# First attention of a hybrid encoder layer: inverse row sums by way of DRAM, another order of the key halves, value products between the scores and both turned tiles

## The reference, cut to what matters

```python
logits = jnp.einsum('bhqd,bhkd->bhqk', q_i, k).astype(jnp.float32) * scale
logits = logits + c_i[..., :, None] - cum[..., None, :]
logits = jnp.where(pos_i[:, None] >= kpos[None, :], logits, -jnp.inf)
p = jax.nn.softmax(logits, axis=-1)
return jnp.einsum('bhqk,bhkd->bhqd', p.astype(v.dtype), v)
```

## Time and profile before

| what | value |
|---|---|
| median of 3 runs | 1885.44 us (1884.57 to 1885.84) |
| the profiled execution | 1884.72 us, of which its span is 1883.0 us |
| PE busy in the span | 1855.8 us (99%) |
| DVE, ACT, POOL busy | 1180.3 us (63%), 765.0 us (41%), 842.1 us (45%) |
| pair 1: first `scores` of pair 1 to that of pair 2 | 801.94 to 852.30, 50.36 us |
| last `normalise` of pair 3 ends | 942.76 us |

### The profile page before, as it was taken

How to read it: one execution, slowest core, us unless ns; L and a number is a source line. 1 busy time by engine, 2 the same in 40 slices (tenths; PEclk the granted TensorE clock), 3 DMA queues, 4 the chain that set the end, 5 groups by cost and what they waited for, 6 DMA issues and landing times.

```text
span 1883.0 us, 25321 instructions
## 1 busy us (share of the span) xinstructions
PE 1855.8 (99%) x9100; PEld 1527.1 (81%) x9100; DVE 1180.3 (63%) x1763; ACT 765.0 (41%) x1439; POOL 842.1 (45%) x635
## 2 busy tenths in 40 slices
PE   7999999999999999999999999999999999999998
PEld 6888888888888878777788888878888888888886
DVE  6966777676777882555604567486534454368778
ACT  5633233332444552555513555353333323334445
POOL 1688877883000111222222332699877887700003
PEclk8999999999999999999999999999999999999999
DMA  9247566654976301301112123524322422178662
GB/s 355 87 140 214 180 209 198 192 167 150 397 226 197 116 24 51 138 18 44 68 56 63 48 65 134 175 89 134 105 91 92 133 99 98 46 295 313 208 190 90
DMA packets 213363, 267.95 MB, mean 142 GB/s; under 512 B 16084, under 2 KB 126840, under 8 KB 212728
## 3 DMA queue, kind: packets, MB, share of 16 engines
q1 hardware_dynamic: 212392, 263.72, 42.2%
q10 hardware_dynamic: 848, 2.62, 0.4%
HBM read 211.17 MB, written 53.03 MB: 140 GB/s over the span
## 4 chain that ended last, share of the span: by engine, by line
PE 88%; POOL 4%; DVE 4%; issue 2%; ACT 1%; DMA 1%; SPq 0%; DVEq 0%; ACTq 0%; POOLq 0%
PE bank L1772 13%; PE bank L1774 13%; PE bank L1773 13%; PE bank L1200 7%; PE bank L1199 7%; PE bank L1201 6%; PE bank L2136 5%; PE bank L2138 5%; PE bank L2137 5%; PE bank L2907 2%; PE bank L2891 2%; PE bank L2876 1%; POOL out_xn L157 1%; PE bank L3304 1%; PE bank L3303 1%
## 5 line engine op out<-in xcount | busy, mean ns | idle before, releaser
L510 POOL TENSOR_TENSOR ffn_ring_b<-ffn_raw_in,ffn_ring_b 128x512 fp32r<-128x512 f32 x146 | 205.6, 1416 | 97.6 <-ACT ffn_ring_b L505 97.5
L1199 PE MATMUL bank<-ffn_w_hi,ffn_a_hi 128*128 128x512 f32 x616 | 239.7, 389 | 0.0
L1201 PE MATMUL bank<-ffn_w_hi,ffn_a_lo 128*128 128x512 f32 x616 | 239.6, 389 | 0.0
L1200 PE MATMUL bank<-ffn_w_lo,ffn_a_hi 128*128 128x512 f32 x616 | 239.6, 389 | 0.0
L132 POOL TENSOR_SCALAR rms<-rms 128x1 f32<-128x1 f32 x20 | 9.0, 450 | 427.6 <-ACT ffn_junk L124 419.6
L1154 ACT CAST ffn_a_hi<-ffn_a_stage 128x512 fp32r<-128x512 f32 x154 | 95.7, 621 | 200.8 <-PE bank L1201 196.9
L505 ACT CAST ffn_ring_b<-ffn_raw_in 128x512 fp32r<-128x512 f32 x150 | 92.5, 621 | 201.9 <-PE bank L1774 195.9
L510 POOL TENSOR_TENSOR ffn_ring_a_lo<-ffn_raw_in,ffn_ring_a_hi 128x512 fp32r<-128x512 f32 x106 | 146.6, 1394 | 54.0 <-ACT ffn_ring_a_hi L505 51.9
L1165 DVE TENSOR_TENSOR ffn_a_lo<-ffn_a_stage,ffn_a_hi 128x512 fp32r<-128x512 f32 x154 | 106.5, 691 | 71.9 <-ACT ffn_a_hi L1154 71.9
L1551 DVE TENSOR_TENSOR ffn_u<-bank,ffn_u 128x512 f32<-128x512 f32 x103 | 70.9, 689 | 109.6 <-PE bank L1774 109.1
L2128 POOL TENSOR_TENSOR mx_w_lo<-mx_raw_w,mx_w_hi 128x1024 fp32r<-128x1024 f32 x25 | 59.8, 2391 | 176.8 <-ACT mx_w_hi L1890 113.3
(11 more groups left out here) (427 smaller groups left out, 4686.9 us busy)
## 6 DMA issues: line engine op xcount, KB each, us to landing
ffn_raw_in<-in_w_ffn_in SPq DMA_DIRECT2D x84, 512.0 KB, 5.8
ffn_a_stage<-hidden SPq DMA_DIRECT2D x154, 256.0 KB, 3.4
ffn_w_stage<-in_w_ffn_out SPq DMA_DIRECT2D x132, 256.0 KB, 3.1
ada_rest<-in_w_ada SPq DMA_DIRECT2D x64, 448.0 KB, 3.9
hidden<-ffn_u SPq DMA_DIRECT2D x87, 256.0 KB, 2.0
hidden<-ffn_g SPq DMA_DIRECT2D x66, 256.0 KB, 2.0
mx_raw_w<-in_w_mix_in SPq DMA_DIRECT2D x28, 512.0 KB, 4.5
x_spill<-xres SPq DMA_DIRECT2D x16, 512.0 KB, 5.6
```

Of the source, the lines that this page charges most:

```text
L510: pool.tensor_tensor(self.lo(q), self.source(b, m), self.hi(q).bitcast(F32), ALU.subtract)\
L1199: pe.matmul(dst, a_hi, w_hi, start=first, stop=False, skip_group_check=True)
L1200: pe.matmul(dst, a_hi, w_lo, start=False, stop=False, skip_group_check=True)
L1201: return pe.matmul(dst, a_lo, w_hi, start=False, stop=True, skip_group_check=True)
```

## The change

Three things are changed together.

1. **The division.** DVE takes the inverse of two numbers per query (128x2) into a table `mx_rinv` of 128 queries by 16. At the end of a pair it transposes the table in 32x32 blocks. SP writes it to DRAM in four small DMAs and reads it back spread over the partitions in two (`spread_inverse`), and POOL multiplies the whole pair's result, 128x1024, in place (`divide`): for pairs 0 to 2 at step 4 of the next pair, for pair 3 after the weight cuts and ahead of the memset of `mx_mask_m`. `turn_rinv` and `keep_rinv` are gone; DVE copies the undivided value product (`keep_y_fox`).
2. **The key halves.** The low half of the keys (g = 2) is projected after step 6 and the high half (g = 3) last. `scores(0)` waits for each half of the keys ahead of its own matmuls. Since the low half is still read by `scores(7)` of the pair before, ACT waits for that ahead of its copy.
3. **The order on PE.** In steps 2 to 5 too, `values(q-2)` stands ahead of both turned tiles.

```diff
@@ -2079,7 +2081,11 @@
-    rinv = core.at("mx_rinv", [P, 4, P], 120)
+    TURN = 32
+    rinv = core.at("mx_rinv", [P, TURN], 120)
+    rinv_rows_in = core.at("mx_rinv_rows_in", [P, TURN], 120.5)
+    rinv_bc = core.at("mx_rinv_bc", [P, S], 16)
+    rinv_rows = nc.dram_tensor("rinv_rows", (PAIRS * 2 * S,), F32, kind="Internal").ap()
@@ -2186,8 +2192,8 @@
     BLOCK = [NS - 1 - n // 2 for n in range(PER)]
-    STEP_OF = {5: 1, 6: 3, 7: 2}
-    QK_ORDER = (1, 3, 2, 0)
+    STEP_OF = {5: 1, 6: 2, 7: 3}
+    QK_ORDER = (1, 2, 3, 0)
@@ -2199,7 +2205,7 @@
-        return core.bank[:, (7, 1, 1, 3)[g], :]
+        return core.bank[:, (7, 1, 3, 1)[g], :]
@@ -2216,6 +2222,21 @@
+
+        def spread_inverse(pairs):
+
+            before = pairs - 1
+            sp.wait_ge(rinv_turned, pairs)
+            rows = rinv_rows[bass.ds(before * (2 * S), 2 * S)].rearrange("(n t) -> n t", t=P)
+            for at in range(0, P, TURN):
+                sp.dma_start(rows[:, at:at + TURN], rinv_rows_in[at:at + 2 * NS, :]).then_inc(rinv_stored, 16)
+            sp.wait_ge(rinv_stored, pairs * (P // TURN * 16))
+            sp.wait_ge(x_spilled, NS * 16)
+            if pairs > 1:
+                sp.wait_ge(y_divided, pairs - 1)
+            for e in range(2):
+                sp.dma_start(rinv_bc[e * HD:(e + 1) * HD, :],
+                             rinv_rows[bass.ds(before * (2 * S) + e * S, S)].partition_broadcast(HD)).then_inc(rinv_loaded, 16)
@@ -2225,13 +2246,19 @@
                     w_load(sp, slot, p + (C_F[slot] + 1), w_in[:, :, bass.ds(p * P + (col + P), P)])
+            if not first and not last:
+                spread_inverse(p)
             if first:
 ...
-        repeat(sp, PAIRS, fox_loads)
+        for p in range(PAIRS):
+            fox_loads(p, p == 0, p == PAIRS - 1)
         for piece in range(4):
             w_load(sp, piece % 2, C_MV[0] + piece // 2, w_in[:, 2 * piece:2 * piece + 2, COL_MV:COL_MV + MW])
+            if piece == 1:
+                spread_inverse(PAIRS - 1)
+        spread_inverse(PAIRS)
@@ -2291,9 +2318,18 @@
+        def divide(pairs):
+
+            part = yT_fox[:, bass.ds(pairs + -1, 1), :].rearrange("p a s -> p (a s)")
+            pool.wait_ge(y_done, pairs * NS)
+            pool.wait_ge(rinv_loaded, pairs * 32)
+            pool.tensor_tensor(part, part, rinv_bc[:, :], ALU.mult).then_inc(y_divided, 1)
+
 ...
                 mask_block(p, q)
+                if q == 4 and not first:
+                    divide(p)
                 if q in (1, 2):
@@ -2318,7 +2354,7 @@
-        pool.wait_ge(y_done, PAIRS * NS)
+        divide(PAIRS)
         pool.memset(mask_m[:, :], 0.0).then_inc(late_mask_set, 1)
@@ -2377,6 +2413,8 @@
             else:
+                if g == 2 and not (isinstance(p, int) and p == 0):
+                    act.wait_ge(score_ready, p * PER)
                 act.copy(fk_hi[:, half], qk_bank(p, g)).then_inc(fq_kept, 1)
@@ -2395,12 +2433,6 @@
-
-        def keep_rinv(p, q, first):
-            act.wait_ge(pv_ready, p * NS + (q + 1))
-            if not (first and q < 2):
-                act.wait_ge(y_done, p * NS + (q - 1))
-            act.copy(rinv[:, 2 + q % 2, :], core.bank[:, 6 + q % 2, P:2 * P]).then_inc(rinv_kept, 1)
@@ -2420,11 +2452,8 @@
                         keep_qk(p + 1, STEP_OF[q - 1])
-                if q > 1:
-                    keep_rinv(p, q - 2, first)
                 if q < NS:
                     keep_pt(p, 2 * q - 1, first)
-            keep_rinv(p, NS - 1, first)
             if not last:
@@ -2613,17 +2643,17 @@
             dve.wait_ge(prob_done, p * PER + (2 * q + 2))
-            if not (first and q < 2):
-                dve.wait_ge(pv_ready, p * NS + (q - 1))
-            dve.reciprocal(rinv[:, q % 2, :].rearrange("p (e d) -> p e d", e=2),
-                           rowsum[:, 2 * q:2 * q + 2].unsqueeze(2).to_broadcast([P, 2, HD]))\
-                .then_inc(rinv_made, 1)
-
-        def normalise(p, q):
-            dve.wait_ge(rinv_kept, p * NS + (q + 1))
             i = BLOCK[2 * q]
-            dve.tensor_tensor(yT_fox[:, bass.ds(p, 1), i * P:(i + 1) * P].rearrange("p a s -> p (a s)"),
-                              core.bank[:, 6 + q % 2, 0:P], rinv[:, 2 + q % 2, :], ALU.mult).then_inc(y_done, 1)
+            inverse = rinv[:, 0:2 * NS].rearrange("p (e i) -> p e i", e=2)[:, :, i:i + 1]
+            if q == 0 and not first:
+                dve.wait_ge(rinv_turned, p)
+            dve.reciprocal(inverse, rowsum[:, 2 * q:2 * q + 2].unsqueeze(2)).then_inc(rinv_made, 1)
+
+        def keep_y_fox(p, q):
+            dve.wait_ge(pv_ready, p * NS + (q + 1))
+            i = BLOCK[2 * q]
+            dve.tensor_copy(yT_fox[:, bass.ds(p, 1), i * P:(i + 1) * P].rearrange("p a s -> p (a s)"),
+                            core.bank[:, 6 + q % 2, 0:P]).then_inc(y_done, 1)
@@ -2642,8 +2672,12 @@
                 if q > 1:
-                    normalise(p, q - 2)
-            normalise(p, NS - 1)
+                    keep_y_fox(p, q - 2)
+            dve.wait_ge(rinv_made, p * NS + NS)
+            if not first:
+                dve.wait_ge(rinv_stored, p * (P // TURN * 16))
+            dve.transpose(rinv_rows_in[:, :], rinv[:, :]).then_inc(rinv_turned, 1)
+            keep_y_fox(p, NS - 1)
             if not last:
@@ -2652,6 +2686,8 @@
         dve.tensor_copy(m_max[:, :], max_turned_bank[:, FH * NS:]).then_inc(max_kept, 1)
+        dve.memset(rinv[:, :], 0.0).then_inc(rinv_set, 1)
+        dve.wait_ge(rinv_set, 1)
         repeat(dve, PAIRS, fox_body)
@@ -2820,9 +2856,9 @@
         def project_qk(p, g, ks=range(KD)):
-            if g % 2:
+            if g in (1, 2):
                 pe.wait_ge(w_lo_done[g // 2], p + (C_F[g // 2] + 1))
-            if g == 2 and ks[0] == 0:
+            if g == 3 and ks[0] == 0:
                 pe.wait_ge(fq_cut, p * 4 + 1)
@@ -2859,16 +2895,16 @@
             heads = [slice(e * HD, (e + 1) * HD) for e in range(2)]
-            if q == 0:
-                pe.wait_ge(fq_cut, p * 4 + 3)
-                if first:
-                    pe.wait_ge(rows_kept, 2)
+            if q == 0 and first:
+                pe.wait_ge(rows_kept, 2)
             if BLOCK[2 * q] == NS // 2 - 1:
 ...
                 k0, k1 = b * BANK, min((b + 1) * BANK, w)
+                if q == 0:
+                    pe.wait_ge(fq_cut, p * 4 + (2 + b))
@@ -2904,13 +2940,9 @@
                 for e in range(2):
-                    pe.matmul(bank[e * HD:(e + 1) * HD, 0:P], v_fox[:, j, bass.ds(p * (2 * HD) + e * HD, HD)],
-                              pt_of(2 * q + e, j * P, (j + 1) * P), start=(j == 0), stop=(j == i))
-
-        def turn_rinv(p, q):
-            bank = core.bank[:, 6 + q % 2, :]
-            pe.wait_ge(rinv_made, p * NS + (q + 1))
-            pe.transpose(bank[:, P:2 * P], rinv[:, q % 2, :], core.ident[:, :]).then_inc(pv_ready, 1)
+                    mm = pe.matmul(bank[e * HD:(e + 1) * HD, 0:P], v_fox[:, j, bass.ds(p * (2 * HD) + e * HD, HD)],
+                                   pt_of(2 * q + e, j * P, (j + 1) * P), start=(j == 0), stop=(j == i))
+            mm.then_inc(pv_ready, 1)
@@ -2922,17 +2954,12 @@
                 scores(p, q, first)
-                if q in (6, 7):
+                if q > 1:
                     values(p, q - 2, first)
-                    turn_rinv(p, q - 2)
                     turn_prob(p, 2 * q - 2, first)
 ...
                     turn_prob(p, 2 * q - 2, first)
-                    if q == 1:
-                        project_q0(p, first, range(KD - 2, KD))
-                    else:
-                        values(p, q - 2, first)
-                        turn_rinv(p, q - 2)
+                    project_q0(p, first, range(KD - 2, KD))
                 turn_prob(p, 2 * q - 1, first)
@@ -2950,8 +2977,6 @@
             values(p, NS - 1, first)
-            turn_rinv(p, NS - 2)
-            turn_rinv(p, NS - 1)
             if not last:
```

More of the change, by code:

```diff
@@ L2032, in mixer @@
     pv_ready, y_done = s("pv_ready"), s("y_done")
-    rinv_made, rinv_kept = s("rinv_made"), s("rinv_kept")
+    rinv_made, rinv_stored, rinv_loaded = s("rinv_made"), s("rinv_stored"), s("rinv_loaded")
+    rinv_set, rinv_turned = s("rinv_set"), s("rinv_turned")
+    y_divided = s("y_divided")
     x_ready, x_kept = s("x_ready"), s("x_kept")
@@ L2492, in ml_body @@
                 act.wait_ge(x_spilled, NS * 16)
+                act.wait_ge(y_divided, PAIRS)
                 for k in range(PAIRS):
@@ L2849, in tensor @@
         project_qk(0, 1, range(2, KD))
-        project_qk(0, 3)
+        project_qk(0, 2)
         pe.wait_ge(rows_ready, 1)
@@ L2853, in tensor @@
                      core.ident[:, :]).then_inc(rows_turned, 1)
-        project_qk(0, 2)
+        project_qk(0, 3)
         def scores(p, q, first):
```

## The result

| | before | changed |
|---|---|---|
| median of 12 runs each | 1884.99 us (1884.38 to 1886.09) | 1890.43 us (1889.59 to 1891.68) |
| span of the profiled execution | 1883.0 us | 1888.7 us |

The ratio is 1.0028, with a 95% interval of 1.0021 to 1.0036: the changed kernel is 5.4 us slower. The forecast was 4.5 us slower.

The account below looks back on a forecast made before the run. PE, busy for 99% of the span, was taken as the bound. The terms -5.1 + 10.7 - 1.4 - 1.1 + 0.8 + 0.6 gave +4.5 us, 1889.9 us on the median's footing, range 1886.0 to 1895.0.

Parts of the forecast that it names:

- The second tile's wait: Steps 2 to 4 of four pairs: PE waits for ACT's copy of the first turned tile, 0.89 each, +10.7 us.
- saved changes of kind: Steps 2 to 5: both tiles form one run of transposes, 0.09 us saved at 15 places, -1.4 us.
- 32 turned inverses at 0.16: Turned inverse sums taken off PE in the attention, 0.16 us from start to start each, -5.1 us.
- The pair's start: First scores no longer wait for the last key half's cut: 0.30 at three places, 0.2 ahead of pair 0, -1.1 us.
- Tile 13's wait: Step 7, pairs 0 to 2: tile 13 waits for ACT's exponentials behind the key half's cast, 0.26 each, +0.8 us.
- Pair 3, step 5: No projection behind it: tile 8 to step 6's value product takes 3.66 us instead of 3.24, +0.6 us in the sum.
- What should cost nothing: DVE's smaller inverse and transpose, ACT's dropped copies, POOL's product, SP's small DMAs: taken as nothing; transpose 0 to +2 us.
- dearer inverses: Rival: each turned inverse on PE costs 0.26 us, 8.3 in all, giving 1886.7 us; chance 0.25.
- The hidden wait: Rival: the wait ahead of the second tile is hidden after all, kernel faster, 1879.2 us; chance 0.05.
- POOL's lock: Rival: POOL's product locks DVE out in step 4, +6 us at three places, 1895.9 us; chance 0.08.
- The late copy: Rival: the last value copy comes late behind DVE's transpose, +1.5, 1891.4 us; chance 0.05.

Follow-up runs that it names:

- part 2 alone: Only the other order of the key halves, put into the kernel before: 1883.31 us, ratio 0.9997.
- ACT's order: New division and key halves with PE's old order, plus ACT making tile 13's exponentials ahead of the key half's cast: 1879.29 us, ratio to before 0.9975.
- part 1 alone: Only the division with inverse sums over DRAM, key halves and PE's order as in the kernel before: 1881.0 us, ratio 0.9984.

## Why the prediction was right, and the term that was not

The forecast was +4.5 us, measured +5.4; its way and mechanism hold, and the size is 0.9 short. It came that near in part by luck: one term gave 1.1 us too much gain, and another 0.5 us too much loss. Point by point:

- **The second tile's wait**, 0.89 each at 12 places, +10.7. Right. The gap from the last transpose to the second tile is 1.01 us in pair 2, and 12 are there. Doubling the copy moves it by the length of the copy. With the saved changes of kind and pair 3's extra the order was forecast at +9.9; it measured +9.4, since a saved change of kind is worth about 0.13 and not 0.09. Pairs 1 and 2 were forecast about 1 us longer, and are 1.18 longer. The term's lower end, 0.72 a place, doesn't follow from the 0.1 that it names (0.89 less 0.1 is 0.79); nothing else rests on it.
- **32 turned inverses at 0.16**, -5.1. This is the step that failed in size. It said that the tile would follow the value product "after the same 0.20 as the inverse does, so 0.16 is what goes". The start does come at the same distance, but the run of transposes behind a value product is 0.05 longer (0.91 for 0.86) than it was behind the inverse. Inside a step 0.11 went, which the prediction had as its lower bound, 18 times in pairs 0 to 2. The two at a pair's end gave 0.37 together once part 2 was there (1.18 to 0.81 us), three times, and pair 3's eight gave 0.89. That is 4.0 us, 1.1 less than forecast.
- **The pair's start**, -1.1. Right: part 2 alone took 0.29 us of wait away where 0.30 was forecast. In the changed kernel the scores follow the value product by 0.81 us, with nothing in brackets:

```profile
854.27 0.88 PE L2943 MATMUL bank<-mx_probT,mx_v_fox 128*64 128x128 f32 x12
855.08 0.50 PE L2912 MATMUL bank<-mx_fk_hi,mx_fq_hi 64*128 64x512 f32 x2
```

  Ahead of pair 0 the gain was 0.12 and not 0.2 (0.44 to 0.32 us from the last projection matmul's start to the scores).
- **Tile 13's wait**, 0.26 at three places. Right: 0.91 for 0.66 us, and ACT's order removes it.
- **Pair 3, step 5**: 3.66 us forecast from the start of the stretch to the value product of step 6; measured 3.65 (933.70 to 937.35).
- **What should cost nothing** did. DVE's transpose took 0.20 us, and the last copy of the value product ended at 907.72, ahead of the query projection behind the scores (which began at 906.62 and take 1.6 us). POOL's product of pair 3 delayed the mask, and DVE's idle time behind that chain fell from 6.91 to 4.57 us, about the 2.4 that were expected. SP issued the first head weights 8 us after the inverse sums, and 5.9 us later than before (953.89), which is how much later the attention ended in this trace.

```profile
907.34 0.20 DVE L2679 STREAM_TRANSPOSE mx_rinv_rows_in<-mx_rinv 128x32 f32<-128x32 f32 x1
907.47 0.25 DVE L2655 COPY mx_yT_fox<-bank 128x128 f32 x1
...
1022.68 0.76 DVE L2758 TENSOR_SCALAR mx_sg<-mx_sg,mx_consts 128x1024 f32<-128x1024 f32 x1 [4.57 <-ACT mx_sg L2510]
```

```profile
951.63 1.09 SPq L2238 DMA_DIRECT2D mx_rinv_bc<-rinv_rows  x2
959.77 0.40 SPq L1879 DMA_DIRECT2D mx_raw_w<-in_w_mix_in  x1
```

Of the rivals, *dearer inverses* is out: part 1 alone is worth 3.0 us, not 8.3; they are cheaper than forecast. *The hidden wait* is out by the twelve rows. *POOL's lock* is out for the logits of the attention, for which it was feared. In the changed kernel POOL's product ran from 877.37 to 879.74; the logits of tile 8 beside it took 0.69 us, as did those of tile 9 behind it:

```profile
877.37 2.37 POOL L2326 TENSOR_TENSOR mx_yT_fox<-mx_yT_fox,mx_rinv_bc 128x1024 f32 x1
...
877.98 0.69 DVE L2629 CUSTOM_DVE_ANT_0 mx_prob<-bank,mx_cum_bc 128x512 f32<-128x512 f32 x1 [0.29 <-issue]
...
880.37 0.69 DVE L2629 CUSTOM_DVE_ANT_0 mx_prob<-bank,mx_cum_bc 128x512 f32<-128x512 f32 x1
```

Behind the attention, where DVE reads SBUF with both inputs, a step of the convolution took 3.30 us beside POOL's weight cut and 1.28 away from it. The Trainium skill (SBUF — State Buffer, "SBUF: two separate sides") says that a VectorE instruction with two SBUF inputs and a GpSimd one that reads SBUF shut each other out. This trace agrees: the step with two SBUF inputs lost 2.0 us beside POOL, and the logits above, with one input in PSUM, lost nothing.

```profile
1009.48 2.92 POOL L2134 TENSOR_TENSOR mx_w_lo<-mx_raw_w,mx_w_hi 128x1024 fp32r<-128x1024 f32 x1 [5.57 <-ACT mx_w_hi L1890]
...
1010.18 3.30 DVE L2749 SCALAR_TENSOR_TENSOR mx_mkT<-mx_pre_k,mx_consts,mx_mkT 128x1024 f32<-128x1024 f32 x1
...
1016.82 1.28 DVE L2749 SCALAR_TENSOR_TENSOR mx_mqT<-mx_pre_q,mx_consts,mx_mqT 128x1024 f32<-128x1024 f32 x1
```

*The late copy* is out, as said.

## What to carry to other kernels

Work of the bounding engine that stands between the filling of a bank and its reuse is not in the way: it is the cover of the copy. Before moving it, add up the time from the last producer's start over the copy to the reuse (here 1.0 us), and look at what work of the same engine is left beside it. Of a bundle of edits, cost each by itself and at the places where they touch: here two parts gained 3.9 us and the third lost 9.4. What an instruction gives back when it goes is read at its place: here 0.11 us in a step, nothing inside a wait, 0.37 for two ahead of the scores.

## What was not expected of the hardware

A run of seven transposes takes 0.98 or 0.99 us behind the value product, in the six kernels where it follows it without a wait. It took 0.93 behind a turned inverse, in the three kernels that have one. The value product's row says `128*64`, the transposes' `128*128`; whether that is the reason was not tried. And a turned inverse of 0.33 us on PE, 0.16 from start to start, gave back 0.11 inside a step when it was taken out.
